# Moving VectorE's read of a finished projection chunk ahead of the recurrence's piece of the same step

## The chip, the cores and the metric

The kernel runs on one core of one Trainium2 chip. The metric is the device time of one execution in microseconds, the median of several runs.

## The reference

One inference step of a hybrid decoder layer, for a prompt of 1024 tokens and eight sample tokens, all in 32-bit floating point. One normalised input is projected into many features; they feed three branches whose outputs are merged, projected and followed by a feed-forward network.

```python
lru_x, lru_gate, q, cmp_kv, sel_kv, win_kv, ngate, mq, merge = project(x, p)
o_lru, conv_new, h_new = lru_branch(lru_x, lru_gate, ...)   # convolution, gates, scan over time
...
o_nsa = lax.map(block, jnp.arange(T // Q_BLOCK, dtype=jnp.int32))   # attention, 3 key sets
o_mem = mem_attend(mq, mkv)
y = merge_ffn(x, o_lru, o_nsa, o_mem, merge, p)
```

The recurrence is `h[t] = a[t] * h[t-1] + b[t]` for 1024 channels, where `a` and `b` come from two sigmoid gates of a four-tap convolution of `lru_x`; its output is multiplied by the GELU of `lru_gate`.

## The kernel before

The function `attention_and_recurrence` is the joined stage. It does three things at once, and every engine has its own instruction queue, written out in order for it.

- **Attention.** 192 steps, `J` = 0 to 191. A step is one head, one block of 128 queries and one of three key sets (`sel`, `win`, `cmp`). TensorE makes the scores of step J+1 (`scores`, tile `att_S`), later the transposes of the probabilities (`transposes`, `att_tp<-att_pr`) and the products with the values of the step before (`values`, `att_O`). VectorE adds the bias and takes the row maximum (`maxima`, `att_nmx`), gathers the output (`accumulate`) and makes the row's factor (`coefficient`). ScalarE makes the exponential (`probs`, `att_pr`), and behind it copies the transposed probabilities out of PSUM (`copies`, `att_ptr`).
- **Filler.** The projection's last 40 units of 128 features are worked off in between: each unit is three chunks, each chunk 24 matmuls into one PSUM bank (`facc`), cut into four ticks of six. `TICKS` says how many ticks a step holds: four (a whole chunk) in steps 0 to 71, one or two from 72 to 172. There is one bank, so the first matmul of a chunk waits until VectorE has read the chunk before it (`evict(g)`, line 1294, `att_zf<-att_facc`, which multiplies by the row's scale). `chunk_at[g]` is the step in which chunk g is finished.
- **Recurrence.** Four blocks of 256 channels. Each is cut into pieces, one a step at most, with steps between that have none: eight of the convolution (`convolve`, `att_xc`), then by number m: 1 and 2 gate times input, 3 and 4 the factor under the root, 6 and 7, 8 and 9 the scans (line 1382), 11 and 12 the output. ScalarE makes the sigmoids, exponentials, roots and GELU that pieces 1, 3, 6 and 11 wait for. The block's gate products on TensorE (`gate_products`, line 1064) wait for the whole convolution.

TensorE's order in step J is: `scores(J+1)`, gate products if any, the filler of step J, `values(J-1)`, `transposes(J)`. ScalarE's is: `probs(J+1)`, `copies(J)`, then weights, gates and its own piece of the recurrence. VectorE's, before, is: `evict` of the chunk that step J-1 finished, `maxima(J)`, `accumulate(J-2)`, `coefficient(J-1)`, the recurrence's piece of step J. In `cmp` steps of the first query block (2, 5, 8, 11, 14, 17, 20 and 23) the masked probabilities are made in `coefficient(J)`, in VectorE's step J+1, and `transposes(J)` waits for them. Steps 1 and 4 hold small instructions on the decay rates (lines 1270 to 1287) where a piece would stand. In steps 12, 41 and 70 the last piece of a block's convolution runs, and in the step behind each of these TensorE has that block's first gate products.

Of the kernel before, what the change touches and what calls it, by code (L numbers as in the profile page):

```python
# [742 lines left out]
def attention_and_recurrence(nc, d, per, h_hi, h_lo):  # L743
# [10 lines left out]
    NU = len(UNITS)  # L754
# [3 lines left out]
    def at(J):  # L758
        b, j = J // NJ, J % NJ
        return b, b // 2, j // NH, HALF[j % NH]  # L760

    def tiles(J):
        _, qt, _, (_, br) = at(J)
        return {"sel": (0, qt + 1), "win": (max(0, qt - 4), min(qt + 1, 5)), "cmp": (0, 1)}[br]
# [29 lines left out]
    chunk_at = {t // 4: J for J in ticks for t in ticks[J] if t % 4 == 3}  # L794
# [3 lines left out]
    for n in range(NBLK):  # L798
        W.append(max(unit_at[4 * n + 1] + 4, free))
        e, J = 0, W[n] + 11  # L800
# [11 lines left out]
    LAST = max(NST + 2, END)  # L812

    with ExitStack() as ctx:
# [439 lines left out]
        def _(dve):  # L1254
            chains, lams = [0], [0]

            def chain(ins):
                chains[0] += 1
                ins.then_inc(s_ch, 1)
                dve.wait_ge(s_ch, chains[0])  # L1260
# [6 lines left out]
            def decay_begin():  # L1267
                L = par[:, :, L_LAM]
                dve.wait_ge(par_in, 32)
                lam_chain(dve.tensor_scalar(lam[:, 0], L, -1.0, None, ALU.mult))  # L1270
                lam_chain(dve.tensor_tensor(lam[:, 1], L, lam[:, 0], ALU.max))
                dve.tensor_scalar(lam[:, 2], lam[:, 0], 0.0, None, ALU.max).then_inc(lam_done, 1)

            def decay_rates():
                dve.wait_ge(lam_ex, 1)
                lam_chain(dve.tensor_scalar(lam[:, 4], lam[:, 3], 2.0, None, ALU.add))
                lam_chain(dve.reciprocal(lam[:, 4], lam[:, 4]))
                lam_chain(dve.tensor_tensor(lam[:, 4], lam[:, 3], lam[:, 4], ALU.mult))
                lam_chain(dve.tensor_tensor(lam[:, 5], lam[:, 4], lam[:, 4], ALU.mult))
                lam_chain(dve.memset(lam[:, 6], 1.0 / 19))  # L1280
                for x in range(17, 0, -2):
                    lam_chain(dve.tensor_tensor(lam[:, 6], lam[:, 6], lam[:, 5], ALU.mult))
                    lam_chain(dve.tensor_scalar(lam[:, 6], lam[:, 6], 1.0 / x, None, ALU.add))
                lam_chain(dve.tensor_tensor(lam[:, 6], lam[:, 6], lam[:, 4], ALU.mult))
                lam_chain(dve.scalar_tensor_tensor(lam[:, 6], lam[:, 6], 2.0, lam[:, 2], ALU.mult, ALU.add))
                lam_chain(dve.tensor_scalar(lam[:, 6], lam[:, 6], -8.0, None, ALU.mult))
                dve.tensor_scalar(lam[:, 7], lam[:, 6], -1.0, None, ALU.mult).then_inc(lam_done, 1)

            def evict(g):
                u, c = g // 3, g % 3  # L1290
                if g >= 4:
                    dve.wait_ge(f_out[g % 4], 16 * (g // 4))
                dve.wait_ge(f_mm, g + 1)
                dve.tensor_tensor(zf[:, g % 4], facc[:, 0:CW], per["rstd"][:, c * CW:(c + 1) * CW],  # L1294
                                  ALU.mult).then_inc(f_ev, 1)

            def maxima(J):
                b, qt, s, (g, br) = at(J)
                x, n, rr = S[J % 2], width(J), 2 * (b % 2) + s
                if J % NH == 0:  # L1300
                    gt = per["gate"][:, qt, :].rearrange("p (g r c) -> p g r c", g=G, r=R)
                    chain(dve.tensor_copy(gsl[:, s], gt[:, :, rr, :]))
                dve.wait_ge(s_mm, J + 1)
                if br == "cmp":
                    c0 = 56 - 8 * qt
                    f = max(0, 40 - c0)
                    chain(dve.tensor_tensor(x[:, f:n], x[:, f:n], cstrip[:, g, rr, c0 + f - 40:c0 + n - 40], ALU.add))
                else:
                    m = min(n, 2 * P)
                    chain(dve.tensor_tensor(x[:, n - m:n], x[:, n - m:n], near[:, g, rr, 2 * P - m:], ALU.add))  # L1310
                    if br == "win" and qt >= 4:
                        chain(dve.tensor_tensor(x[:, 0:P], x[:, 0:P], wmask[:], ALU.add))
                dve.tensor_reduce(nmx[:, J % 2:J % 2 + 1], x[:, 0:n], AX, ALU.max, negate=True).then_inc(s_max, 1)  # L1313

            def coefficient(J):
                _, qt, s, (g, br) = at(J)
                bi = ("cmp", "sel", "win").index(br)
                v = rs[:, J % 2:J % 2 + 1]
                dve.wait_ge(s_exp, J + 1)
                if br == "cmp" and qt == 0:  # L1320
                    pm = pr[:, J % 2, 0:NCMP]
                    dve.tensor_tensor(pm, pm, cmask[:], ALU.mult).then_inc(s_pm, 1)  # L1322
                    dve.wait_ge(s_pm, J // 3 + 1)
                    chain(dve.tensor_reduce(v, pm, AX, ALU.add))
                    chain(dve.tensor_scalar(v, v, 1e-30, None, ALU.max))
                chain(dve.reciprocal(cf[:, J % 2, 0:1], v))
                chain(dve.tensor_tensor(cf[:, J % 2, 1:2], cf[:, J % 2, 0:1], gsl[:, s, g, bi:bi + 1], ALU.mult))

            def accumulate(J):
                _, _, s, (g, br) = at(J)  # L1330
                dve.wait_ge(s_pvg, vgroup(J + 1, 0))
                o = oacc[:, s, g * HD:(g + 1) * HD]
                c = cf[:, J % 2, 1:2]
                if br == "sel":
                    dve.tensor_scalar(o, O[:, 0:HD], c, None, ALU.mult).then_inc(s_acc, 1)
                else:
                    dve.wait_ge(s_acc, J)
                    dve.scalar_tensor_tensor(o, O[:, 0:HD], c, o, ALU.mult, ALU.add).then_inc(s_acc, 1)
# [20 lines left out]
            def recurrence(n, k, m):  # L1359

                if 2 <= k <= 9:
                    convolve(n, k - 2)
                if m in (1, 2):
                    t = m - 1
                    dve.wait_ge(sg_done, n + 1)
                    dve.tensor_tensor(ig[:, t], ig[:, t], xc[:, t], ALU.mult).then_inc(u_done, 1)
                if m in (3, 4):
                    t = m - 3
                    dve.wait_ge(a2_done, 2 * n + t + 1)
                    dve.scalar_tensor_tensor(e_[:, t], r[:, t], 1.0, e_[:, t], ALU.add, ALU.mult).then_inc(th_done, 1)  # L1370
                if m in (6, 7):
                    t = m - 6
                    dve.wait_ge(rt_done, n + 1)
                    dve.wait_ge(u_done, 2 * n + t + 1)
                    dve.tensor_tensor(ig[:, t], ig[:, t], e_[:, t], ALU.mult).then_inc(b_done, 1)
                if m in (8, 9):
                    t = m - 8
                    dve.wait_ge(b_done, 2 * n + t + 1)
                    dve.tensor_tensor(r[:, t, NP_:T], a[:, t, NP_:T], st[:, 2 * n + t, 3 * NS:], ALU.mult).then_inc(hs_done, 1)
                    dve.wait_ge(hs_done, 2 * n + t + 1)  # L1380
                    dve.tensor_tensor(r[:, t, NP_:T], r[:, t, NP_:T], ig[:, t, NP_:T], ALU.add)
                    dve.tensor_tensor_scan(r[:, t, 0:NP_], a[:, t, 0:NP_], ig[:, t, 0:NP_], 0.0, ALU.mult, ALU.add).then_inc(sc_done, 1)
                if m in (11, 12):
                    t = m - 11
                    dve.wait_ge(gl_done, n + 1)
                    dve.wait_ge(sc_done, 2 * n + t + 1)
                    dve.tensor_tensor(ig[:, t], r[:, t], e_[:, t], ALU.mult).then_inc(y_done, 1)
# [10 lines left out]
            chain(dve.tensor_copy(cstrip[:].rearrange("p g r n -> p (g r) n")[:, :, 0:24],  # L1398
                                  strip.rearrange("p h (n x) -> p h n x", x=16)[:, :, :, 0]))
            for J in range(LAST):  # L1400
                for g in range(3 * NU):
                    if chunk_at[g] + 1 == J and J:
                        evict(g)
                if J < NST:
                    maxima(J)
                if 2 <= J < NST + 2:
                    accumulate(J - 2)
                if 1 <= J <= NST:
                    coefficient(J - 1)
                if J == 1:  # L1410
                    decay_begin()
                if J == 4:
                    decay_rates()
                for n in range(NBLK):
                    recurrence(n, J - W[n], J - SIG[n])
            for g in range(3 * NU):
                if chunk_at[g] + 1 >= LAST:
                    evict(g)


# [1150 lines left out]
```

## Time and profile before

| | us |
|---|---|
| median of 3 runs | 2594.26 (2590.0 to 2599.5) |
| profiled execution | 2596.29 |
| its span, first to last instruction | 2594.6 |
| mean granted TensorE clock | 0.951 |
| TensorE busy | 2391.7 |
| VectorE busy | 1098.1 |
| ScalarE busy | 719.1 |

The profiled execution is one execution, 2.0 us above the median. Its span is what the views show; 1.7 us lie around it. Engines run side by side, so the busy times do not add up. The joined stage's steps 0 to 138 lie from 427.9 to about 1132 us of the span; the last recurrence piece is in step 137.

### The profile page before, as it was taken

What the parts mean: (1) busy time and instruction counts of PE and PEld (TensorE: products, weight loads), DVE (VectorE), ACT (ScalarE), POOL (GpSimd) and SP (SyncE); (2) the same over time, 40 slices, a digit from 0 to 9 for tenths busy, and PEclk for the clock granted to TensorE, in tenths of its full rate; (3) what the DMA queues carried; (4) which work ended last, traced back from release to release, by engine and by line L of the source; (5) the groups of instructions that cost most, each with busy time, mean ns of one, the idle gap of its engine ahead of it and who ended that gap; (6) DMA issues with size and microseconds to landing.
All of it is one profiled execution on the core that took longest, in us unless ns stands there. A gap on an engine that the chain in (4) does not pass through costs nothing. (4 is left out here: it accounts for less than half of the span.)

```text
span 2594.6 us, 37768 instructions
## 1 busy us (share of the span) xinstructions
PE 2391.7 (92%) x14375; PEld 2186.5 (84%) x14375; DVE 1098.1 (42%) x1981; ACT 719.1 (28%) x1319; POOL 648.9 (25%) x388
## 2 busy tenths in 40 slices
PE   7997777889989989989967899799999999999999
PEld 7996547878889778889856576799999999999999
DVE  5465013525336374465436221663333333333333
ACT  5222012133243544544334100432211111111111
POOL 2112102112211011111004120135443434434343
PEclk9998699999989999999868999899999999999999
DMA  5223506225534131120035332642111111111112
GB/s 178 88 80 133 177 29 191 63 70 177 135 84 116 39 100 40 42 88 29 20 110 132 122 114 90 220 147 98 42 49 42 49 40 49 43 46 49 40 49 81
DMA packets 135963, 226.31 MB, mean 87 GB/s; under 512 B 30842, under 2 KB 93946, under 8 KB 135228
## 3 DMA queue, kind: packets, MB, share of 16 engines
q1 hardware_dynamic: 118172, 191.50, 24.2%
q0 software_dynamic: 5376, 21.00, 2.4%
q10 hardware_dynamic: 12288, 12.06, 1.6%
q8 instruction: 85, 1.39, 0.2%
q14 instruction: 42, 0.34, 0.0%
HBM read 176.80 MB, written 55.08 MB: 89 GB/s over the span
## 5 line engine op out<-in xcount | busy, mean ns | idle before, releaser
L1114 PE MATMUL att_facc<-h_hi,att_w_hi 128*128 128x344 f32 x960 | 338.3, 352 | 57.3 <-DVE att_zf L1294 44.2
L1114 PE MATMUL att_facc<-h_hi,att_w_lo 128*128 128x344 f32 x960 | 315.1, 328 | 0.0
L1114 PE MATMUL att_facc<-h_lo,att_w_hi 128*128 128x344 f32 x960 | 315.0, 328 | 0.0
L2275 PE MATMUL tl_acc<-tl_x_hi,up_w_hi 128*128 128x344 f32 x1248 | 266.1, 322 | 16.1 <-DVE tl_x_lo L2338 13.6
L2275 PE MATMUL tl_acc<-tl_x_lo,up_w_hi 128*128 128x344 f32 x1248 | 265.7, 321 | 0.0
L2275 PE MATMUL tl_acc<-tl_x_hi,up_w_lo 128*128 128x344 f32 x1248 | 264.0, 320 | 0.0
L2240 POOL TENSOR_TENSOR up_w_lo<-up_raw,up_w_hi 128x1024 fp32r<-128x1024 f32 x64 | 154.0, 2407 | 424.9 <-ACT up_w_hi L2180 424.9
L1114 PEld LDWEIGHTS att_facc<-h_hi,att_w_hi 128*128 128x128 f32 x960 | 188.3, 196 | 71.8 <-DVE att_zf L1294 41.9
L1152 ACT ACTIVATE att_pr<-att_S,att_nmx 128x63 f32<-128x63 f32 (+8 forms) x192 | 110.0, 573 | 474.1 <-DVE att_nmx L1313 473.8
L1009 POOL TENSOR_TENSOR att_w_lo<-att_raw,att_w_hi 128x1024 fp32r<-128x1024 f32 x40 | 98.0, 2450 | 558.9 <-ACT att_w_hi L1147 558.9
L2392 DVE TENSOR_TENSOR up_z<-tl_acc,up_z 128x1032 f32<-128x1032 f32 x176 | 217.0, 1233 | 47.8 <-PE tl_acc L2325 46.8
L2180 ACT ACTIVATE up_w_hi<-up_raw 128x1024 fp32r<-128x1024 f32 x64 | 68.0, 1062 | 597.4 <-PE tl_acc L2275 390.6
L2275 PEld LDWEIGHTS tl_acc<-tl_x_hi,up_w_hi 128*128 128x128 f32 x1248 | 210.1, 188 | 17.3 <-issue 16.9
L2275 PEld LDWEIGHTS tl_acc<-tl_x_lo,up_w_hi 128*128 128x128 f32 x1248 | 212.0, 190 | 0.0
L2275 PEld LDWEIGHTS tl_acc<-tl_x_hi,up_w_lo 128*128 128x128 f32 x1248 | 208.5, 188 | 0.0
L1114 PEld LDWEIGHTS att_facc<-h_lo,att_w_hi 128*128 128x128 f32 x960 | 188.7, 197 | 8.1 <-issue 7.7
L1114 PEld LDWEIGHTS att_facc<-h_hi,att_w_lo 128*128 128x128 f32 x960 | 187.8, 196 | 0.0
L1294 DVE TENSOR_TENSOR att_zf<-att_facc,h_rstd 128x344 f32<-128x344 f32 x120 | 61.8, 515 | 293.9 <-PE att_facc L1114 293.5
L1077 PE MATMUL att_tp<-per_ident,att_pr 128*128 128x128 f32 x592 | 108.1, 297 | 15.8 <-DVE att_pr L1322 15.8
L2325 PE MATMUL tl_acc<-up_x_hi,up_w_hi 128*128 128x344 f32 x528 | 121.4, 338 | 0.0
L2388 DVE TENSOR_TENSOR tl_tmp<-tl_acc,tl_tmp 128x1032 f32<-128x1032 f32 x22 | 27.1, 1233 | 220.9 <-PE tl_acc L2275 214.7
L1164 ACT ACTIVATE att_ptr<-att_tp 63x128 f32<-63x128 f32 (+4 forms) x256 | 98.5, 410 | 67.7 <-PE att_tp L1077 67.1
(375 smaller groups left out, 4494.0 us busy)
## 6 DMA issues: line engine op xcount, KB each, us to landing
up_raw<-in_w_ff SPq DMA_DIRECT2D x66, 512.0 KB, 3.6
z<-att_zf SPq DMA_DIRECT2D x120, 172.0 KB, 4.1
att_raw<-in_w_in SPq DMA_DIRECT2D x40, 512.0 KB, 4.2
tl_tmp<-z SPq DMA_DIRECT2D x24, 516.0 KB, 6.0
fr_raw<-in_w_in SPq DMA_DIRECT2D x14, 512.0 KB, 4.8
zn<-fr_x SPq DMA_DIRECT2D x10, 516.0 KB, 2.9
fr_x<-in_xT SPq DMA_DIRECT2D x8, 644.0 KB, 10.4
up_raw<-in_w_up ACTq DMA_DIRECT2D x10, 512.0 KB, 3.7
```

Of the source, the lines that this page charges most:

```text
L1009: pool.tensor_tensor(w_lo[:, u % 2], raw[:, u % 2], w_hi[:, u % 2].bitcast(F32), ALU.subtract).then_inc(f_lo, 1)
L1077: mm = pe.transpose(tp[tg % 2][:, (t % 4) * P:(t % 4 + 1) * P], pr[:, J % 2, t * P:(t + 1) * P], per["ident"][:])
L1114: mm = pe.matmul(facc[:, 0:CW], w[:, u % 2, k, :], h[:, k, c * CW:(c + 1) * CW], start=(x == 0), stop=(x == 23))
L1152: act.activation(pr[:, J % 2, 0:n], S[J % 2][:, 0:n], ACT.Exp, bias=nmx[:, J % 2:J % 2 + 1], accum_out=rs[:, J % 2:J % 2 + 1]).then_inc(s_ ...
L1164: act.activation(ptr[0:w, vg % 4, 0:m], tp[tg % 2][0:w, 0:m], ACT.Copy).then_inc(s_te, 1)
L1294: dve.tensor_tensor(zf[:, g % 4], facc[:, 0:CW], per["rstd"][:, c * CW:(c + 1) * CW], ALU.mult).then_inc(f_ev, 1)
L2180: act.activation(w_hi[:, u % 2], raw[:, u % 2], ACT.Copy).then_inc(whi_done, 1)
L2240: pool.tensor_tensor(w_lo[:, u % 2], raw[:, u % 2], w_hi[:, u % 2].bitcast(F32), ALU.subtract).then_inc(wlo_done, 1)
L2275: mm = pe.matmul(a[:, c, 0:CW], wt[:, s, k, :], x[:, x0, c * CW:(c + 1) * CW], start=first and n == 0, stop=last and n == 2)
L2325: mm = pe.matmul(acc[m % 2][:, c, 0:CW], wt[:, j, m, :], x[:, j, c * CW:(c + 1) * CW], start=(n == 0), stop=(n == 2))
L2388: dve.tensor_tensor(gj, acc[1][:, :, 0:CW], gj, ALU.mult).then_inc(ev_done, 1)
L2392: dve.tensor_tensor(chunks(h[:, m]), acc[m % 2][:, :, 0:CW], chunks(h[:, m]), ALU.add).then_inc(ev_done, 1)
```

## The change

VectorE's read of a chunk moves from the beginning of step J+1 to step J itself, between `coefficient(J-1)` and the recurrence's piece (or the decay instructions). Since nothing else stands between the end of step J and the beginning of step J+1, only the piece is passed.

```diff
             for J in range(LAST):
-                for g in range(3 * NU):
-                    if chunk_at[g] + 1 == J and J:
-                        evict(g)
                 if J < NST:
                     maxima(J)
                 if 2 <= J < NST + 2:
                     accumulate(J - 2)
                 if 1 <= J <= NST:
                     coefficient(J - 1)
+                for g in range(3 * NU):
+                    if chunk_at[g] == J:
+                        evict(g)
                 if J == 1:
                     decay_begin()
                 if J == 4:
                     decay_rates()
                 for n in range(NBLK):
                     recurrence(n, J - W[n], J - SIG[n])
             for g in range(3 * NU):
-                if chunk_at[g] + 1 >= LAST:
+                if chunk_at[g] >= LAST:
                     evict(g)
```

Of the 114 chunks that are finished in steps 0 to 172, 57 end in a step with a piece or decay instructions, and for these the order changes; for the other 57 it is what it was. The other engines' queues do not change.

VectorE's queue around step 8, a `cmp` step of the first query block with a piece of the convolution (lines 1356 and 1357); `att_pr` in line 1322 are the masked probabilities of step 8. Before:

```order
L1327 TENSOR_TENSOR att_cf<-att_cf,att_gsl 128x1
L1356 SCALAR_TENSOR_TENSOR att_xc<-att_xp,att_par,att_xc 128x1024
L1357 SCALAR_TENSOR_TENSOR att_xc<-att_xp,att_par,att_xc 128x8
L1294 TENSOR_TENSOR att_zf<-att_facc,h_rstd 128x344
L1310 TENSOR_TENSOR att_S<-att_S,att_near 128x128
L1313 TENSOR_REDUCE att_nmx<-att_S 128x1
L1338 SCALAR_TENSOR_TENSOR att_oacc<-att_O,att_cf,att_oacc 128x64
L1322 TENSOR_TENSOR att_pr<-att_pr,att_cmask 128x63
```

The same place now:

```order
L1327 TENSOR_TENSOR att_cf<-att_cf,att_gsl 128x1
L1294 TENSOR_TENSOR att_zf<-att_facc,h_rstd 128x344
L1356 SCALAR_TENSOR_TENSOR att_xc<-att_xp,att_par,att_xc 128x1024
L1357 SCALAR_TENSOR_TENSOR att_xc<-att_xp,att_par,att_xc 128x8
L1310 TENSOR_TENSOR att_S<-att_S,att_near 128x128
L1313 TENSOR_REDUCE att_nmx<-att_S 128x1
L1338 SCALAR_TENSOR_TENSOR att_oacc<-att_O,att_cf,att_oacc 128x64
L1322 TENSOR_TENSOR att_pr<-att_pr,att_cmask 128x63
```

The chunk's read (line 1294) has passed the convolution's two instructions; these now stand between it and the next step's maxima and mask.

VectorE's queue around step 57, which holds piece 6 of block 1 (line 1375, behind ScalarE's square root). Before:

```order
L1327 TENSOR_TENSOR att_cf<-att_cf,att_gsl 128x1
L1375 TENSOR_TENSOR att_ri<-att_ri,att_e 128x1032
L1294 TENSOR_TENSOR att_zf<-att_facc,h_rstd 128x344
L1310 TENSOR_TENSOR att_S<-att_S,att_near 128x256
L1313 TENSOR_REDUCE att_nmx<-att_S 128x1
```

Now:

```order
L1327 TENSOR_TENSOR att_cf<-att_cf,att_gsl 128x1
L1294 TENSOR_TENSOR att_zf<-att_facc,h_rstd 128x344
L1375 TENSOR_TENSOR att_ri<-att_ri,att_e 128x1032
L1310 TENSOR_TENSOR att_S<-att_S,att_near 128x256
L1313 TENSOR_REDUCE att_nmx<-att_S 128x1
```

Here the read no longer stands behind an instruction that waits for ScalarE, and the maxima of step 58 still do.

## Rows read from the trace of the kernel before

**Rows 1.** The page: busy time, share of the span, instructions, of TensorE.

```profile
PE 2391.7 (92%) x14375; PEld 2186.5 (84%) x14375; DVE 1098.1 (42%) x1981; ACT 719.1 (28%) x1319; POOL 648.9 (25%) x388
```

**Rows 2.** TensorE's waits (total us, times, longest) in 427.9:560, 560:847.6, 847.6:1139 in turn.

```profile
PE att_tp L1077 <- DVE att_pr L1322: 10.3, 7, 1.6
...
PE att_facc L1114 <- DVE att_zf L1294: 13.6, 7, 4.0
...
PE att_facc L1114 <- DVE att_zf L1294: 19.1, 7, 5.7
...
PE att_O L1096 <- ACT att_ptr L1164: 6.3, 9, 1.2
```

**Rows 3.** Busy time by stretch, instructions, granted clock, DMA share, GB/s.

```profile
core 0: us, PE busy (x) PEld busy (x) DVE busy (x) ACT busy (x) POOL busy (x), PEclk, DMA share, GB/s
...
560.00:847.60 287.60, 268.48 (x1658) 252.22 (x1658) 136.14 (x377) 108.15 (x229) 58.26 (x48) 0.96 0.44 122
...
847.60:1139.00 291.40, 265.75 (x1700) 238.08 (x1699) 163.23 (x441) 149.39 (x323) 33.02 (x21) 0.96 0.21 64
```

**Rows 4.** Timeline, step 57: start, us, engine, line, operation [idle before].

```profile
766.22 0.32 PE L1114 MATMUL att_facc<-h_hi,att_w_lo 128*128 128x344 f32 x1
...
768.78 1.23 DVE L1375 TENSOR_TENSOR att_ri<-att_ri,att_e 128x1032 f32<-128x1032 f32 x1 [5.15 <-ACT att_e L1207]
...
770.49 0.66 PE L1114 MATMUL att_facc<-h_hi,att_w_hi 128*128 128x344 f32 x1 [2.96 <-DVE att_zf L1294]
...
771.97 0.48 ACT L1164 ACTIVATE att_ptr<-att_tp 128x384 f32<-128x384 f32 x1
...
776.88 0.55 PE L1096 MATMUL att_O<-att_v_sel,att_ptr 128*128 128x64 f32 x4
```

**Rows 5.** Timeline after steps 33 and 52: ScalarE's copy, TensorE's value products.

```profile
630.17 0.37 ACT L1164 ACTIVATE att_ptr<-att_tp 128x256 f32<-128x256 f32 x1
...
634.34 0.55 PE L1096 MATMUL att_O<-att_v_sel,att_ptr 128*128 128x64 f32 x4
...
741.40 0.48 ACT L1164 ACTIVATE att_ptr<-att_tp 128x384 f32<-128x384 f32 x1
...
746.67 0.55 PE L1096 MATMUL att_O<-att_v_win,att_ptr 128*128 128x64 f32 x4
```

**Rows 6.** Timeline after step 81, where the next filler is two ticks long.

```profile
896.92 0.65 PE L1114 MATMUL att_facc<-h_hi,att_w_hi 128*128 128x344 f32 x1 [5.65 <-DVE att_zf L1294]
...
898.64 0.59 ACT L1164 ACTIVATE att_ptr<-att_tp 128x512 f32<-128x512 f32 x1
...
900.53 0.73 PE L1096 MATMUL att_O<-att_v_sel,att_ptr 128*128 128x64 f32 x3
```

**Rows 7.** Timeline of step 8: convolution, chunk read, masked probabilities, transpose.

```profile
472.86 1.28 DVE L1356 SCALAR_TENSOR_TENSOR att_xc<-att_xp,att_par,att_xc 128x1024 f32<-128x1024 f32 x1
...
474.06 0.22 DVE L1357 SCALAR_TENSOR_TENSOR att_xc<-att_xp,att_par,att_xc 128x8 f32<-128x8 f32 x1
...
476.17 0.52 DVE L1294 TENSOR_TENSOR att_zf<-att_facc,h_rstd 128x344 f32<-128x344 f32 x1 [1.88 <-PE att_facc L1114]
...
477.59 0.33 PE L1077 MATMUL att_tp<-per_ident,att_pr 128*128 128x128 f32 x1 [1.37 <-DVE att_pr L1322]
```

**Rows 8.** Timeline of step 13: the recurrence's first gate products.

```profile
498.11 0.68 PE L1064 MATMUL att_S<-att_xc,att_wa 128*128 128x512 f32 x1
```

**Rows 9.** VectorE by line, 427.9:1139: busy us, mean ns of one, idle before.

```profile
L1382 DVE TENSOR_TENSOR_SCAN att_ri<-att_xp,att_ri 128x1024 f32<-128x1024 f32 x8 | 18.3, 2284 | 0.0
```

**Rows 10.** Timeline after step 134, a scan step: copy and value products.

```profile
1119.25 0.26 ACT L1164 ACTIVATE att_ptr<-att_tp 63x128 f32<-63x128 f32 x1
...
1119.65 0.40 PE L1096 MATMUL att_O<-att_v_cmp,att_ptr 63*128 63x64 f32 x2 [0.42 <-ACT att_ptr L1164]
```

**Rows 11.** Two fillers, 24 matmuls each: after waits of 2.48 and 1.57 us.

```profile
455.00:460.40 5.40, 5.40 (x24) 5.40 (x25) 1.74 (x7) 0.58 (x3) 0.00 (x0) 0.68 0.17 38
...
493.50:497.40 3.90, 3.90 (x27) 3.73 (x25) 3.79 (x5) 1.22 (x2) 2.49 (x1) 1.00 0.00 0
```

## The prediction

> **What bounds the kernel now.** I began with the page: TensorE is busy for 92% of the span [rows 1], so a change on VectorE can give or take only what TensorE waits. The change touches steps 1 to 136, and I asked next for TensorE's waits in three stretches of these (steps 0 to 21, 22 to 71, 72 to 138). The reader sees three kinds [rows 2]. TensorE waits for the read of the last chunk (13.6 and 19.1 us in the second and third stretch): that is what the change can remove. In the first it waits for masked probabilities (10.3 us, the `cmp` steps). And in the third it waits for ScalarE's copies (6.3 us), the other end of the chain maxima, exponential, copy. The granted clock in the last two stretches is 0.96 [rows 3], so low-clock time is small but there. Then I read the timeline at single steps, since each moved read has its own answer: what stood behind it, and which wait ends last afterwards.
>
> **What the change removes.** It adds no instruction; what counts is what the read no longer waits for, and what now waits for the read.
>
> Step 57 is the clear case. The filler's last matmul starts at 766.22, but VectorE stands until 768.78 before a piece that waits for ScalarE's root (5.15 us idle); the read comes behind it, and TensorE starts the next filler at 770.49 after 2.96 us [rows 4]. Afterwards the read comes at about 766.7, and TensorE goes on at 770.49 - 2.96 = 767.5. A filler of four ticks takes 3.9 us at full clock [rows 11], so it ends at 771.4. Then the value products need ScalarE's copy, behind the exponential and the maxima, and these are still behind the piece. They come only 0.42 us earlier, since the read (0.52 us, the next instruction 0.43 behind it) is no longer ahead of them: the copy ended at 771.97 + 0.48 = 772.45 and will end at 772.0. The products start at 772.05 instead of 776.88 [rows 4]: **4.8 us**, of which 2.5 are not the wait itself but the filler at half clock behind it.
>
> The same with steps 33 and 52: copies end at 630.54 and 741.88, less 0.42; the products started at 634.34 and 746.67 [rows 5]. That is 4.2 and 5.2 us. The other waits of this stretch are 13.6 less the three long ones (2.98, 3.96, 2.96), so 3.7 us; the four-tick filler covers the chain behind them, and I take them whole. Step 23, where the transposes wait anyway, gives the 0.4 of the read. Second stretch: **18.1 us given back**.
>
> In the third stretch a filler is one or two ticks, so it hides much less of the same chain. At step 81 the wait is 5.65 us, but the copy ended at 899.23 and the products started at 900.53 [rows 6]: 900.53 - 898.85 = 1.7 us is all that is won, and the rest becomes a wait for ScalarE. Read in the same way, the other five places with a long wait (steps 86, 91, 126, 131 and 136) give 1.6, 2.4, 0.5, 0.5 and 1.0. Third stretch: **7.7 us**, 0.4 of its 19.1.
>
> **What it adds.** The read waits for TensorE's filler of the same step, and the piece is behind it in VectorE's queue. Before, the piece ran in the time in which VectorE had nothing to do (idle 1.88 us before the read at step 8, with the piece done [rows 7]); that cover is gone. The piece now starts after the filler's end, and the maxima, the mask and the gate products wait for it. Four prices follow.
>
> (a) Steps 5, 8 and 11: the transposes wait for the mask made behind the piece. At step 8 TensorE waited 1.37 us, from the read at 476.17 to 477.59; the piece (474.06 + 0.22 - 472.86 = 1.42 us) comes in between [rows 7]. So 1.4 us each at 8 and 11, with waits of 2.8 and 3.0 us. After a wait of 2.48 us the filler ran at a mean clock of 0.68 for 5.4 us (partly at 1.2 instead of 2.4 GHz), and after one of 1.57 us at 1.00 [rows 11]: (1 - 0.68) x 5.4 = 1.7 us lost. Waits of 2.8 to 3.0 us are on the far side, so I add 1.7 us to each: 6.2 us. At steps 4 and 5 the decay instructions (28 small ones in step 4, some 5 us) move behind the read: the filler starts 2.5 us sooner and then waits as much behind them, at both places without work, for 1.5 us more of low clock. Sum 7.7 us.
>
> (b) Steps 12, 41 and 70: gate products in the next step wait for the convolution. The first starts at 498.11 [rows 8]; the filler of step 12 ends at 497.5, then read and piece take 0.5 + 1.4 us, so 499.5. 1.4, 1.4 and, with longer transposes ahead, 0.8: 3.6 us.
>
> (c) The scans, 2.28 us and with their small instructions 2.6 [rows 9]. In four-tick steps the copy ended 2.0 to 2.3 us before the value products began, so 0.3 to 0.6 is left over, at steps 30, 59 and 60: 1.3 us. Other pieces (1.2 to 1.5 us) fit under the filler in these steps, about thirty times, at no cost. If that cover were 1 us shorter, each would cost up to 0.5 us.
>
> (d) In the third stretch pieces fit less well. At step 134 the copy ended at 1119.51 and the products began at 1119.65 [rows 10]; the scan ran while the filler did and now starts behind it, 1.6 us later. That is 1.4 us. Steps 83, 88, 93, 95 and 129, read alike, give 0.8, 1.0, 1.3, 0.85 and 0.25. Sum 5.6 us.
>
> The Trainium skill ("TensorE: Matmul & The Clock Gate", "Architectural detail: the array is 16× 32×32, not 1× 128×128", on queue depths) says that VectorE and ScalarE are strict first-in, first-out, while TensorE may at most pull weight loads ahead. That speaks against this change: by this rule a read that waits for TensorE also holds a piece whose inputs are ready. The trace agrees, with reads behind waiting pieces in every case above.
>
> **Sum.** First stretch: 7.7 + 1.4 = 9.1 us longer. Second: 18.1 - (1.4 + 0.8 + 1.3) = 14.6 shorter. Third: 7.7 - 5.6 = 2.1 shorter. In all 7.6 us shorter, against the profiled execution of 2596.29: 2588.7. That one is 2.0 us above the median, so on the median 2594.26 it is 2586.7; I say **2587**. What follows step 138 has its own order and moves along as it is.
>
> **The rivals.**
>
> *The clock doesn't fall in steps 8 and 11* and the small pieces cost nothing. For it: a low stretch is not certain, after 1.57 us there was none [rows 11]. Then 3.4 of (a), 1.5 of steps 4 and 5 and some 3 us of (d) are not lost: 15 to 16 us shorter, 2579. Chance 0.17.
>
> *The wait only moves.* TensorE stands as long for ScalarE's copies as it did for the read. For it: this is what step 81 shows, and 70% of the third stretch. Against it: steps 33, 52 and 57, where a filler of 3.9 us lies between. It would need the long fillers to gain only their waits (9.9 instead of 14.2) and 3 us more of (d): within 1 us of no change, 2594. Chance 0.20.
>
> *Slower: pieces without cover.* The one mechanism is (c) with a cover that is too short: VectorE's queue after a filler's end is read 0.5, piece 1.5, maxima 0.5 to 1.1, then exponential and copy, and the next read is due one filler later. If these about thirty-five steps lose 0.5 us each, it is 17 us against the 7.6: 2604. It decides from 0.2 us a step. Against it: the copies are 2.0 us or more ahead there, and the piece takes 1.5. Chance 0.11.
>
> *The change does nothing* cannot be: 57 reads change place.
>
> **How the numbers follow.** The forecast has 0.52, with a range of its own from 2581 to 2592 (the clock at steps 5, 8 and 11 both ways, the third stretch half as large or twice). A measurement of this kernel can tell about 0.3% from no change, that is 7.8 us: below 2586.5 is faster. That line runs through the middle of my forecast: 0.26 of it is faster, 0.26 the same. With the first rival faster is 0.43; with the second, and none from the third, same is 0.46; slower is 0.11. The range for 8 in 10 takes in the first rival and the second whole and leaves the third out: 2577 to 2599.
>
> **What the profile after would show.** If right: TensorE's waits for the chunk's read in the second stretch fall from 13.6 to under 2 us; in the third from 19.1 to under 4, while the waits for ScalarE's copies rise from 6.3 to some 17. Waits for the masked probabilities in the first stretch rise from 10.3 to 13 or more, with two or three waits near 3 us and low clock behind them. From step 0 to step 22 it takes 9 us longer, from there to step 72 15 us less, and from there to step 138 2 us less. If the low clock is missing there, the first rival holds. If the second stretch gives less than 10 us, the step that failed is the cover of ScalarE's chain by the long filler. The prediction is wrong above all if ScalarE's own pieces, which I moved along with the rest, come to stand between exponential and copy.

## The result, and the profile after

| | before | after |
|---|---|---|
| median of 20 runs each, on one chip | 2594.89 (2590.0 to 2602.92) | **2603.74** (2593.98 to 2611.09) |
| ratio | | **1.0032** (95%: 1.0022 to 1.0042) |
| profiled execution; its span | 2596.29; 2594.6 | 2599.66; 2598.0 |

The change makes the kernel 8.9 us slower; the forecast was 7.6 us faster. The profiled execution of after lies 4.1 us below the median of its kernel, that of before 1.4 us above its own. So the two profiles differ by only 3.4 us, and a reading of the whole spans would hide most of the loss.

The page's line of busy times, beside [rows 1]:

```profile
PE 2386.9 (92%) x14375; PEld 2179.8 (84%) x14375; DVE 1101.6 (42%) x1981; ACT 718.1 (28%) x1319; POOL 651.9 (25%) x388
```

TensorE is busy for 4.8 us less than before, and the span is 3.4 us longer: it waits more. Where, is told by the windows, cut at the first filler matmul of steps 0, 22, 72 and 138 (width; busy us by engine; granted clock; DMA share and GB/s):

```profile
core 0: us, PE busy (x) PEld busy (x) DVE busy (x) ACT busy (x) POOL busy (x), PEclk, DMA share, GB/s
429.21:567.34 138.13, 119.69 (x688) 107.88 (x688) 49.80 (x201) 27.94 (x90) 21.85 (x12) 0.96 0.27 77
567.34:849.73 282.39, 265.27 (x1660) 247.08 (x1659) 144.73 (x377) 108.31 (x229) 60.55 (x48) 0.99 0.44 126
849.73:1140.03 290.30, 263.37 (x1649) 236.59 (x1648) 157.83 (x427) 145.40 (x313) 31.07 (x21) 0.94 0.19 58
```

The same steps took 132.05, 287.63 and 283.37 us before. The last column of the next table is half of the time in which the clock records stand at 0.5 (1.2 instead of 2.4 GHz), that is what the low clock costs at most.

| steps | before | after | difference | forecast | low clock, before and after |
|---|---|---|---|---|---|
| 0 to 21 | 132.05 | 138.13 | +6.1 | +9.1 | 3.4, 5.1 |
| 22 to 71 | 287.63 | 282.39 | -5.2 | -14.6 | 11.9, 3.4 |
| 72 to 137 | 283.37 | 290.30 | +6.9 | -2.1 | 11.9, 17.1 |
| sum | 703.05 | 710.82 | +7.8 | -7.6 | |

The rest of the 3.4 us lies where the order is that of before: the start lies 1.2 us later, and steps 174 to 190 took 57.54 us instead of 63.41, at a granted clock of 0.79 instead of 0.66.

Each of these lengths is from one profile. How far they scatter is told by the profiles of the experiments below, where several kernels have one VectorE order in a stretch. The first took 130.5 to 132.1 us in eight with the order of before, and 137.7 to 138.1 in after, e2, e5 and e7, which move the reads that the forecast prices there. The third took 281.1 to 287.0 us in seven with the order of before (low clock 11.9 to 17.1 us), and 289.5 to 290.4 in three with that of after. So the third stretch is longer for sure, but by how much is uncertain by some 3 us.

TensorE's waits in the same three stretches, in turn (total us, times, longest), beside [rows 2]:

```profile
PE att_tp L1077 <- DVE att_pr L1322: 13.3, 7, 2.9
...
PE att_O L1096 <- ACT att_ptr L1164: 10.5, 11, 2.0
...
PE att_facc L1114 <- DVE att_zf L1294: 0.2, 1, 0.2
...
PE att_O L1096 <- ACT att_ptr L1164: 26.7, 14, 5.6
```

The waits for the chunk's read are gone, 13.6 and 19.1 us before and 0.2 and none now. In their place TensorE waits for ScalarE's copies: 10.5 us in the second stretch, where there was no such wait before, and 26.7 in the third.

Step 57, timeline, beside [rows 4] (start, us, engine, line, operation, idle before):

```profile
768.77 0.40 PE L1114 MATMUL att_facc<-h_hi,att_w_hi 128*128 128x344 f32 x1
...
770.13 1.23 DVE L1375 TENSOR_TENSOR att_ri<-att_ri,att_e 128x1032 f32<-128x1032 f32 x1 [1.53 <-ACT att_e L1207]
...
772.91 0.48 ACT L1164 ACTIVATE att_ptr<-att_tp 128x384 f32<-128x384 f32 x1
...
773.53 0.63 PE L1096 MATMUL att_O<-att_v_sel,att_ptr 128*128 128x64 f32 x4 [0.75 <-ACT att_ptr L1164]
```

This went as forecast. The next filler starts at 768.77 without a wait, and the value products start 0.14 us behind the copy's end (773.39). From the filler's start of step 57 to these products it took 14.26 us before and 9.50 now: 4.8 us. Steps 33 and 52 [rows 5], measured alike, give 4.1 and 5.1.

Step 8, beside [rows 7]:

```profile
479.21 0.52 DVE L1294 TENSOR_TENSOR att_zf<-att_facc,h_rstd 128x344 f32<-128x344 f32 x1 [2.04 <-PE att_facc L1114]
...
479.65 1.28 DVE L1356 SCALAR_TENSOR_TENSOR att_xc<-att_xp,att_par,att_xc 128x1024 f32<-128x1024 f32 x1
...
481.70 0.21 DVE L1322 TENSOR_TENSOR att_pr<-att_pr,att_cmask 128x63 f32<-128x63 f32 x1
...
481.98 0.48 PE L1077 MATMUL att_tp<-per_ident,att_pr 128*128 128x128 f32 x1 [2.73 <-DVE att_pr L1322]
```

The convolution runs between the read and the mask, and the wait for the mask is 2.73 us instead of 1.37.

### The profile page after: what moved, and what is told of

The parts are those of the page before. It is cut to its first block and busy times, and to the rows that moved or that the text cites. A ratio compares the mean times of both kernels' runs of the same rounds, so it can differ in the third digit from the quotient of the medians.

```text
span 2598.0 us, 37726 instructions
## 1 busy us (share of the span) xinstructions
PE 2386.9 (92%) x14375; PEld 2179.8 (84%) x14375; DVE 1101.6 (42%) x1981; ACT 718.1 (28%) x1319; POOL 651.9 (25%) x388
## 5 line engine op out<-in xcount | busy, mean ns | idle before, releaser
L1114 PEld LDWEIGHTS att_facc<-h_hi,att_w_hi 128*128 128x128 f32 x960 | 186.9, 195 | 35.1 <-POOL att_w_lo L1009 13.6
L1077 PE MATMUL att_tp<-per_ident,att_pr 128*128 128x128 f32 x592 | 107.5, 295 | 18.3 <-DVE att_pr L1322 18.3
```

What stands on the lines that cost most here:

```text
L1077: mm = pe.transpose(tp[tg % 2][:, (t % 4) * P:(t % 4 + 1) * P], pr[:, J % 2, t * P:(t + 1) * P], per["ident"][:])
L1114: mm = pe.matmul(facc[:, 0:CW], w[:, u % 2, k, :], h[:, k, c * CW:(c + 1) * CW], start=(x == 0), stop=(x == 23))
```

## Experiments

Each kernel ran beside the kernel before on the same chip; the ratio has its 95% interval. A step in `early` is one in which the read goes ahead of the piece; in all others the order is that of before:

```diff
                 for g in range(3 * NU):
-                    if chunk_at[g] + 1 == J and J:
+                    if chunk_at[g] + 1 == J and J and J - 1 not in early:
                         evict(g)
...
                     coefficient(J - 1)
+                for g in range(3 * NU):
+                    if chunk_at[g] == J and J in early:
+                        evict(g)
```

The expectations name two theories of the loss. The collision theory: a moved piece meets GpSimd's subtraction and is stretched by it. The cover theory: the chain of piece, maxima, exponential and copy is too long for the filler, with or without GpSimd.

### The change in two halves

```diff
+            early = {SIG[n] + m for n in range(NBLK) for m in (1, 6, 11)}
```

These are the twelve steps whose piece waits for ScalarE (`e1_scalar_pieces`).

> The read goes ahead of the piece only in the 12 steps whose piece waits for ScalarE (m = 1, 6 and 11 of each block); everywhere else it is as before. Both theories say that the gains of the changed kernel are made here and its losses elsewhere: 17 to 19 us less from step 22 to step 72, up to 8 us less behind it, so 15 to 25 us less than before in all. If instead the gains were taken back by waits for ScalarE that follow later, it would be within 5 us of before.

Measured: 2574.84 us against 2593.58, ratio 0.993 (0.9917 to 0.9943), 18.7 us faster. The second stretch took 273.46 us, 14.2 less than before, where the gains of the forecast come to 18.1. Of the missing 3.9, 3.3 lie behind steps 34 and 63, which hold two pieces ahead of the read in this kernel: against after, it starts the next filler 1.2 and 2.1 us later there. The third took 281.63, only 1.7 less, where the forecast had 7.7. TensorE's waits in the third stretch of this kernel:

```profile
PE att_O L1096 <- ACT att_ptr L1164: 21.1, 12, 5.6
PE att_facc L1114 <- DVE att_zf L1294: 0.6, 1, 0.6
```

The 19.1 us for the read have become waits for ScalarE's copies.

```diff
+            early = set(range(LAST)) - {SIG[n] + m for n in range(NBLK) for m in (1, 6, 11)}
```

The complement (`e2_other_pieces`).

> The complement: the read goes ahead in the other 45 steps alone. Collision theory and cover theory both expect a slower kernel, by what the changed kernel lost and e1 won together: 9 + 20 = 25 to 30 us more than before. If it is less than 12 us more, losses and gains do not add up and something else is at work.

Measured: 2609.19 us against 2593.58, ratio 1.0064 (1.0051 to 1.0078), 15.6 us slower, where both theories had 25 to 30: the halves, -18.7 and +15.6, come to -3.1 in sum, and the whole change is +8.9. By stretches it lost 5.8, 9.1 and 5.8 us against before. The first and the third are near what (a), (b) and (d) say. In the second the forecast has 3.5 us for steps 41, 70 and the scans, and everything else there at no cost.

### What makes the pieces longer

In the profile of after, step 36's convolution shows it (GpSimd is POOL):

```profile
646.48 2.38 POOL L1009 TENSOR_TENSOR att_w_lo<-att_raw,att_w_hi 128x1024 fp32r<-128x1024 f32 x1 [11.70 <-ACT att_w_hi L1147]
...
646.64 0.52 DVE L1294 TENSOR_TENSOR att_zf<-att_facc,h_rstd 128x344 f32<-128x344 f32 x1 [1.50 <-PE att_facc L1114]
...
647.07 2.87 DVE L1356 SCALAR_TENSOR_TENSOR att_xc<-att_xp,att_par,att_xc 128x1024 f32<-128x1024 f32 x1
...
649.86 0.21 DVE L1357 SCALAR_TENSOR_TENSOR att_xc<-att_st,att_par,att_xc 128x8 f32<-128x8 f32 x1
...
650.45 0.42 DVE L1313 TENSOR_REDUCE att_nmx<-att_S 128x1 f32<-128x256 f32 x1
...
651.37 0.37 ACT L1164 ACTIVATE att_ptr<-att_tp 128x256 f32<-128x256 f32 x1
...
651.89 0.63 PE L1096 MATMUL att_O<-att_v_sel,att_ptr 128*128 128x64 f32 x4 [0.63 <-ACT att_ptr L1164]
```

GpSimd starts its subtraction on the filler's weights (line 1009) at 646.48. VectorE's read beside it keeps its 0.52 us, but the convolution takes 2.87 us instead of 1.28 and ends at 649.94, 1.09 us behind GpSimd's end. Maxima, exponential and copy come that much later, and TensorE waits 0.63 us. The same place before:

```profile
641.34 1.28 DVE L1356 SCALAR_TENSOR_TENSOR att_xc<-att_xp,att_par,att_xc 128x1024 f32<-128x1024 f32 x1
...
642.65 2.38 POOL L1009 TENSOR_TENSOR att_w_lo<-att_raw,att_w_hi 128x1024 fp32r<-128x1024 f32 x1 [14.49 <-ACT att_w_hi L1147]
...
644.12 0.52 DVE L1294 TENSOR_TENSOR att_zf<-att_facc,h_rstd 128x344 f32<-128x344 f32 x1 [1.35 <-PE att_facc L1114]
...
644.55 0.42 DVE L1310 TENSOR_TENSOR att_S<-att_S,att_near 128x256 f32<-128x256 f32 x1
```

There the convolution was through when GpSimd began, VectorE then waited for the filler, and what ran beside GpSimd was the read and the bias, both from PSUM, at their usual length. VectorE's lines in after show the sum (busy us, mean ns of one, idle before):

```profile
L1356 DVE SCALAR_TENSOR_TENSOR att_xc<-att_xp,att_par,att_xc 128x1024 f32<-128x1024 f32 x24 | 37.2, 1552 | 0.1
...
L1382 DVE TENSOR_TENSOR_SCAN att_ri<-att_xp,att_ri 128x1024 f32<-128x1024 f32 x8 | 18.3, 2284 | 0.0
...
L1370 DVE SCALAR_TENSOR_TENSOR att_e<-att_ri,att_e 128x1032 f32<-128x1032 f32 x8 | 11.4, 1422 | 0.1
...
L1387 DVE TENSOR_TENSOR att_ri<-att_ri,att_e 128x1032 f32<-128x1032 f32 x8 | 11.3, 1417 | 3.0 <-ACT att_e L1210 2.9
```

The means before were 1285, 2284 [rows 9], 1234 and 1232 ns. The Trainium skill ("SBUF — State Buffer", "Who interferes with whom") states that a VectorE instruction with two SBUF inputs contends with a GpSimd instruction that reads SBUF, and that whichever starts first blocks the other wholly, while one with at most one SBUF input does not contend outside the 2-port modes. The trace agrees: the convolution has two inputs in SBUF and is held for all of GpSimd's instruction; the read has one, the other being in PSUM. The other way round is in the trace too. Here a scan, also with two inputs in SBUF, started 0.45 us ahead of the subtraction:

```profile
784.55 2.28 DVE L1382 TENSOR_TENSOR_SCAN att_ri<-att_xp,att_ri 128x1024 f32<-128x1024 f32 x1
...
785.00 4.03 POOL L1009 TENSOR_TENSOR att_w_lo<-att_raw,att_w_hi 128x1024 fp32r<-128x1024 f32 x1 [15.28 <-ACT att_w_hi L1147]
```

The scan kept its 2.28 us, and GpSimd's subtraction took 4.03 us instead of 2.38. The scans' mean did not move.

Two kernels were to move GpSimd's subtraction off the pieces, one on after and one on before:

```diff
                     if unit_at[u - 2] == J:
+                        if J < 6 * NJ:
+                            pool.wait_ge(s_max, J + 3)
                         w_low(u)
```

> The changed kernel, with GpSimd's subtraction of each unit's weights held back in steps 0 to 71 until the row maxima of step J+2 are done, so that it does not run beside a moved piece. Collision theory: VectorE's long pieces are no longer stretched (none over 1.5 us between steps 22 and 72), and that stretch is 8 to 12 us shorter than in the changed kernel, so 8 to 12 us less in all. Cover theory (the chain piece, maxima, exponential, copy is too long for the filler with or without GpSimd): within 3 us of the changed kernel.

> The same delay of GpSimd's subtraction in the kernel before, as a control. Both theories: within 4 us of before, since there the pieces run ahead of the subtraction. If it is as much faster as e3, the delay helps for another reason.

Measured: 2601.85, ratio 1.0039 (1.0025 to 1.0053), and 2608.97, ratio 1.0058 (1.0045 to 1.0071), both against 2593.58. The second stretch of the first took 282.74 us, no less than after's 282.39. The control, which should have stayed within 4 us of before, lost 15.4. The delayed subtraction had found another victim: the small product of the coefficient (line 1327 in before), which has two SBUF inputs too, took 2.2 instead of 0.16 us 23 times in each of these two kernels. So here too the length goes by what lies beside GpSimd, but nothing can be read from the pair about the change.

So the subtraction itself was made small, in after and in before. From unit 2 on it covers 8 elements a partition instead of 1024, so the low part of the filler's weights is left out:

```diff
-                pool.tensor_tensor(w_lo[:, u % 2], raw[:, u % 2], w_hi[:, u % 2].bitcast(F32), ALU.subtract).then_inc(f_lo, 1)
+                k, m = (KT, P) if u < 2 else (1, 8)
+                pool.tensor_tensor(w_lo[:, u % 2, 0:k, 0:m], raw[:, u % 2, 0:k, 0:m],
+                                   w_hi[:, u % 2, 0:k, 0:m].bitcast(F32), ALU.subtract).then_inc(f_lo, 1)
```

> The changed kernel with GpSimd's subtraction cut to 8 columns from the third unit on; it leaves out the low part of these weights, so TensorE works on old values in the same matmuls. Collision theory: no long piece of VectorE is stretched from step 22 to 72, and this stretch takes 270 to 274 us instead of 282.4. Cover theory: 279 us or more, since ScalarE's chain is as long as it was.

> The same cut in the kernel before. Both theories: step 22 to step 72 within 4 us of the 287.6 of before, since there GpSimd runs mostly beside reads of PSUM. So with e5 the change should win 5 us or more as a whole by the collision theory (forecast of the prediction: 7.6), and lose as it did by the cover theory.

Measured: 2590.56, ratio 0.9984 (0.9972 to 0.9997), and 2583.2, ratio 0.9951 (0.9939 to 0.9963), both against 2593.82. Second and third stretch of the first of them, by windows:

```profile
567.39:840.43 273.04, 262.93 (x1659) 245.52 (x1659) 132.10 (x377) 108.03 (x229) 22.94 (x48) 0.99 0.43 128
840.43:1130.85 290.42, 263.67 (x1649) 236.64 (x1648) 150.69 (x424) 144.96 (x312) 11.45 (x21) 0.94 0.19 58
```

Its convolution and its pieces of lines 1370 and 1387 (two lines lower here), and its waits for the copies in the second stretch:

```profile
L1358 DVE SCALAR_TENSOR_TENSOR att_xc<-att_xp,att_par,att_xc 128x1024 f32<-128x1024 f32 x24 | 31.4, 1307 | 0.1
...
L1389 DVE TENSOR_TENSOR att_ri<-att_ri,att_e 128x1032 f32<-128x1032 f32 x8 | 10.0, 1249 | 4.4 <-ACT att_e L1212 4.3
...
L1372 DVE SCALAR_TENSOR_TENSOR att_e<-att_ri,att_e 128x1032 f32<-128x1032 f32 x8 | 9.8, 1226 | 0.1
```

```profile
PE att_O L1098 <- ACT att_ptr L1166: 2.9, 6, 1.0
```

The second stretch takes 273.04 us instead of after's 282.39, the means are back at 1307, 1249 and 1226 ns, and the waits for the copies fall from 10.5 to 2.9 us. In before the same edit gives 285.75 instead of 287.63. So with the small subtraction the change gives 12.7 us in this stretch (forecast 14.6), with the real one 5.2: **7.5 us** is what the interference takes. In the third stretch it explains nothing: 290.42 in this kernel against 290.30 in after. And it does not decide the sign: with the small subtraction on both sides the change still costs 2590.56 - 2583.2 = 7.4 us, 1.5 less than the 8.9 with the real one. The collision theory had the change win 5 us or more as a whole; so it was right for the second stretch and wrong for the whole kernel.

### The terms one at a time

```diff
+            early = {4, 5, 8, 11, 12, 41, 70}
...
+            early = {SIG[n] + m for n in range(2) for m in (1, 6, 11)}
```

The first line is that of e7, the second that of e8.

> The read goes ahead only in steps 4, 5, 8, 11, 12, 41 and 70: the mask and gate prices alone, (a) and (b) of the prediction, 11.3 us together. Both theories: 8 to 13 us slower than before, 6 to 9 of it ahead of step 22. If the low clock behind the two waits near 3 us is only chance, 4 to 8.

> e1 without its six steps behind step 72: the read goes ahead in steps 23, 28, 33, 52, 57 and 62 alone. Both theories: 14 to 18 us faster than before. With e1's 18.7 us the difference shows what the six late steps are worth: 2 to 5 us if most of the wait turns into a wait for ScalarE there, as forecast for step 81; 8 or more if the whole wait were won.

Measured, against 2593.82: 2604.09, ratio 1.0034 (1.0021 to 1.0046), 10.3 us slower; and 2579.59, ratio 0.994 (0.9927 to 0.9952), 14.2 us faster. By the medians the price of the seven steps is about right (11.3 forecast). By stretches e7 is 5.6, 4.7 and 2.6 us longer than before, where the forecast has 9.1, 2.2 and none; the 2.6 lie where its order is that of before. The six waiting pieces of blocks 0 and 1 carry three quarters of what all twelve give; the six in the third stretch are worth 18.7 - 14.2 = 4.5 us by the medians, and 1.7 to 1.9 by the profiles' windows (281.63 against 283.37 and 283.50).

```diff
+            early = {J for J in range(72, LAST)} - {SIG[n] + m for n in range(NBLK) for m in (1, 6, 11)}
...
+            early = ({J for J in range(22, 72)} - {SIG[n] + m for n in range(NBLK) for m in (1, 6, 11)}) - {41, 70}
```

The first line is that of e9, the second that of e10. A third kernel, `e11_second_other_small`, is e10 with the small subtraction, and leaves out the same part of the weights as above.

> The read goes ahead only behind step 72 and only where the piece does not wait for ScalarE (steps 83, 88, 93, 95, 97, 129 and 134; price (d) of the prediction, 5.6 us). Theory that only the pieces' own time is uncovered: 4 to 7 us slower than before. Theory that TensorE's new waits of 1.75 to 2 us bring low clock as well, four spells of 1.7 us: 8 to 13 us slower, with 3 us or more of additional low-clock loss between step 72 and 138.

> The read goes ahead only from step 23 to 69 where the piece does not wait for ScalarE, without 41; the prediction gave these 1.3 us. Collision theory: 8 to 12 us slower than before, all of it between steps 22 and 72. If the pieces fit under the filler as predicted: within 3 us of before.

> e10 with GpSimd's subtraction cut to 8 columns as in e6, its control at 2583.2 us; it leaves out the low part of these weights. Collision theory: within 3 us of e6. Cover theory: as much slower than e6 as e10 is slower than before.

Measured, against 2595.32: e9 2591.46, ratio 0.9986 (0.9977 to 0.9995); e10 2600.49, ratio 1.0019 (1.0003 to 1.0035); e11 2589.94, ratio 0.9973 (0.9964 to 0.9982). e10 is 5.2 us slower by the medians, less than the 8 to 12 expected. But its second stretch took 297.68 us, 10.1 more than before, from steps that the forecast prices at 1.3 us together. TensorE's waits in it:

```profile
PE att_facc L1114 <- DVE att_zf L1294: 12.4, 6, 4.0
PE att_O L1096 <- ACT att_ptr L1164: 7.6, 8, 1.6
```

The waits for the read stay, since the waiting pieces are where they were, and 7.6 us of waits for the copies are added. With the small subtraction the same order takes 286.90 us against 285.75 (e6), 1.1 us more. This is the plainest evidence: the pieces do fit under the filler, as long as GpSimd is not beside them. As a whole e11 is 6.7 us slower than e6, though (1.5 of it in the runs of before on its chip), which its moved steps don't account for: 3.8 us of it lie in the third stretch of the two profiles, where both have the order of before.

In e9 the third stretch and steps 174 to 190 read:

```profile
850.01:1139.37 289.36, 259.86 (x1650) 232.81 (x1648) 156.63 (x426) 145.53 (x313) 31.05 (x21) 0.96 0.19 58
1277.64:1333.18 55.54, 45.70 (x284) 41.92 (x285) 26.11 (x86) 23.92 (x65) 1.46 (x2) 0.83 0.03 7
```

The third stretch is 6.0 us longer than before, as term (d) has it (5.6), without more low clock (11.9 us in both). The second of its two theories had four more spells of low clock there, and none came. And yet the kernel as a whole is 3.9 us faster by the medians. Steps 174 to 190, whose order is the same in all these kernels, took 55.54 us here and 63.41 in before, at a granted clock of 0.83 instead of 0.66. Whether a change in the stretch ahead brings this about, or it is chance, one profile each can't tell.

### A better version

The piece that waits for ScalarE can be moved and the read left where it is: VectorE's pieces m = 1, 6 and 11 are done one step later, together with 2, 7 and 12.

```diff
-                if m in (6, 7):
-                    t = m - 6
+                if m == 7:
                     dve.wait_ge(rt_done, n + 1)
-                    dve.wait_ge(u_done, 2 * n + t + 1)
-                    dve.tensor_tensor(ig[:, t], ig[:, t], e_[:, t], ALU.mult).then_inc(b_done, 1)
+                    dve.wait_ge(u_done, 2 * n + 2)
+                    for t in range(2):
+                        dve.tensor_tensor(ig[:, t], ig[:, t], e_[:, t], ALU.mult).then_inc(b_done, 1)
```

and pieces 1 and 2, and 11 and 12, likewise.

> The kernel before, with its order of the read, but the pieces m = 1, 6 and 11 of each block run one step later, together with m = 2, 7 and 12. VectorE then has no reason to stand before ScalarE's result with a chunk's read and the next row maxima behind it. If the cause of TensorE's long waits is this queueing alone, both the read and the maxima are on time: faster than e1 by another 4 to 12 us, 2562 to 2571 us. If ScalarE itself, busy with its own piece, is what TensorE waits for, it is within 4 us of e1 (2575).

Measured: **2563.43** against 2593.54, ratio 0.9887 (0.9868 to 0.9906), 30 us faster than before and 11.4 faster than e1. Windows of the three stretches:

```profile
432.26:562.82 130.56, 116.69 (x687) 105.28 (x688) 55.00 (x201) 27.90 (x90) 22.30 (x12) 0.99 0.29 84
562.82:829.90 267.08, 261.68 (x1659) 245.87 (x1659) 136.51 (x377) 107.66 (x229) 59.09 (x48) 0.99 0.46 131
829.90:1104.17 274.27, 257.27 (x1650) 230.25 (x1648) 158.74 (x426) 145.11 (x313) 31.08 (x21) 0.96 0.20 61
```

Its waits in the second and the third:

```profile
PE att_facc L1114 <- DVE att_zf L1294: 2.9, 3, 2.4
...
PE att_O L1096 <- ACT att_ptr L1164: 0.6, 1, 0.6
...
PE att_O L1096 <- ACT att_ptr L1164: 16.2, 13, 4.6
```

Some wait for the read is left, 2.9 us, but in the third stretch the waits for the copies are 16.2 us instead of e1's 21.1: the maxima no longer stand behind a waiting piece either.

## Why the prediction was wrong

Between the first filler of step 0 and that of step 138 the forecast had 7.6 us less, and the profiles have 7.8 more. The first stretch came out 3.0 us better than forecast, the second 9.4 worse and the third 9.0 worse.

**Right: what the read waited for, and the gains at it.** Steps 33, 52 and 57 gave 4.1, 5.1 and 4.8 us (forecast 4.2, 5.2 and 4.8), and TensorE's waits for the read fell as told. Adding up each filler start of the second stretch that came sooner against before gives 18.7 us (forecast 18.1, though its own terms, 4.8, 4.2, 5.2, 3.7 and 0.4, add up to 18.3); those that came later, 13.5 (forecast 3.5).

**Right in mechanism, somewhat dear: (a) and (b).** The longest waits for the mask are 2.9 and 2.73 us, and the 2.2 us that the filler starts sooner behind step 4 came back as a wait of 2.4 us. Low clock followed at steps 5 and 8, with spells of 6.8 and 3.4 us. Steps 4 and 5 together cost 1.7 us (forecast 1.5), step 8 2.9 (3.1), step 11 1.4 (3.1, no low clock), the gate products behind step 12 1.5 (1.4): 7.5 us instead of 9.1. That the stretch as a whole is only 6.1 us longer has another reason: before has a low-clock spell at 554.2, behind the wait for the mask of step 20, worth 1.5 us, which after, e2, e5 and e7 don't have. Seven of the eight profiles with the order of before in these steps have it, so it seems to go with that order; why, is open.

What did not hold is the premise, "Waits of 2.8 to 3.0 us are on the far side". The wait of 2.93 us at step 11 had no low clock behind it, in after and in e2, e5 and e7 alike. And [rows 11]'s own case, a wait of 2.46 to 2.49 us ahead of step 5's filler in eight kernels, had low clock behind it in before, e6 and e8 and none in e1, e9, e10, e11 and e12. The forecast priced low clock at steps 8 and 11 as certain, and it came at 8 alone.

**The step that failed: (c), "Other pieces (1.2 to 1.5 us) fit under the filler in these steps, about thirty times, at no cost".** I looked at how long the pieces take and how long the filler covers them, and didn't ask what runs beside the pieces at their new place. Before, VectorE did them while it would else have been idle, and met GpSimd's subtraction mostly with instructions that read PSUM. Now they begin 0.43 us behind the read, and some meet it. A few of them pay, as the filler starts of after and e5 show, set side by side: after is later by 1.5 us at the start of step 32's filler, 0.9 at 38, 0.9 at 41, 0.8 at 56, 2.8 and 0.5 at 65 and 66, 1.3 at 68 and 0.8 at 71. That is 9.5 us (7.5 net of what the small subtraction gives before), for the most part from pieces two steps ahead of each (at 65 up to 1.7 of the 2.8 us is a low-clock spell behind the longer wait, at 806.2): the value products that wait for the copy stand between. The cause is shown by e5 and e6, and by e10 and e11, in which 10.1 us become 1.1. The forecast's own guard named this outcome, "If the second stretch gives less than 10 us, the step that failed is the cover of ScalarE's chain by the long filler". The cover fell short because the piece was longer, and not because the filler was shorter.

**Mis-sized: the third stretch, -2.1 us forecast, +6.9 measured.** Term (d) was right within the scatter: 5.6 forecast, 6.0 in e9. The gain of 7.7 us was not: e1 shows 1.7, and the medians of e1 and e8 4.5. Step 81 in after, beside [rows 6]:

```profile
898.65 0.59 ACT L1164 ACTIVATE att_ptr<-att_tp 128x512 f32<-128x512 f32 x1
...
899.38 1.94 PE L1096 MATMUL att_O<-att_v_sel,att_ptr 128*128 128x64 f32 x8 [5.64 <-ACT att_ptr L1164]
...
902.82 0.49 PE L1114 MATMUL att_facc<-h_hi,att_w_hi 128*128 128x344 f32 x1
...
903.11 0.49 PE L1114 MATMUL att_facc<-h_lo,att_w_hi 128*128 128x344 f32 x1
```

The products start 1.6 us sooner after the filler of step 81 than before, as forecast (1.7); the same in e1. But before, the low clock behind the wait fell on the filler of step 82, and that of step 83 had full clock again, 2.04 us for its 12 matmuls. Now TensorE does filler 82 first, then waits 5.64 us, and the low clock falls on the products and on filler 83: its matmuls start 0.29 us apart instead of 0.16. In e1 filler 83 takes 3.63 us, and at the start of filler 84 nothing of the 1.7 us is left; the kernel is 0.8 us behind there. Step 126 went the same way: 1.1 us won, 2.0 lost within two steps. I had counted only up to the value products, and carried no cost for the clock behind a wait that stays. Low clock in the third stretch is 11.9 us before, 13.7 in e1 and 17.1 in after; of the 6.9 us that this stretch took longer, up to 5.2 are low clock. That share is weak evidence, since e4 has 17.1 with the order of before there. What makes after's 17.1 out of e1's 13.7 and e9's 11.9 stays open: the additions of e9 alone cost 6.0 us, on top of e1 8.7.

**The rivals.** *The wait only moves* is what the third stretch did, and more than that; the 70% that the prediction gives for the stretch is step 81's share, by its own sum it is 60%. *Pieces without cover* gives 2604, within 0.3 us of the result, but that is chance: it had 0.5 us at thirty-five steps, and the runs show 0.5 to 2.8 us at eight, no cover missing elsewhere (e11), and the rest of the loss in the third stretch. *The clock doesn't fall* holds at step 11 alone. The check that I set, that ScalarE's copies would take up the waits from 6.3 to some 17, went to 26.7.

**What does not add up.** In the stretches where they moved reads, e1, e7, e9 and e10 together give +5.6, +0.6 and +4.3 us against before, 10.5 in sum; the change gives +6.1, -5.2 and +6.9, 7.8 in sum. By medians it is worse: -18.7, +10.3, -3.9 and +5.2, in sum -7.1, against +8.9 measured, as the two halves gave -3.1. So each term's mechanism is read from its steps, and the sizes are good to a few microseconds only. The difference lies in part in steps 174 to 190, 55.5 to 64.5 us long in kernels with one order there.

## What to carry to other kernels

When an instruction is moved in a queue, look up what every other engine does at its new time, GpSimd above all: an instruction with both inputs in SBUF that is moved off idle time may wait for the rest of a GpSimd instruction that began before it. Follow a gain past the wait that it removes to the end of the next two steps, since low clock that followed the wait before can follow the one that takes its place. And if one instruction in a queue waits long, move that one and leave those that don't: the twelve waiting pieces one step later gave 30 us, where the read ahead of every piece cost 9.

## What the runs showed of the hardware

- VectorE instructions as small as 128x1 and 128x8 are held too. In before, at the place below, one that usually takes 0.16 us takes 1.26 beside a subtraction of GpSimd from 921.73 to 924.10; a `TENSOR_SCALAR` of 128x8 with one SBUF tensor took 2.33 instead of 0.28 us beside another, at 801.95.

```profile
922.86 1.26 DVE L1327 TENSOR_TENSOR att_cf<-att_cf,att_gsl 128x1 f32<-128x1 f32 x1
```

- It goes both ways: in before, GpSimd's subtraction that started at 609.46 beside a scan running from 608.44 took 3.4 us instead of 2.38, and the scan its usual 2.28.
- The length of one wait of TensorE did not settle whether low clock followed. None followed a wait of 2.93 us until 500.55 in after, one of 1.94 until 788.86 in e1 and one of 1.76 until 602.02 in before; it did follow waits of 1.75 us until 935.73 and of 1.94 until 1129.10, both in after.
- Executions of kernels with the same order in steps 174 to 190 differ there by up to 9 us, with the granted clock of these steps between 0.63 (e10, 64.50 us) and 0.83 (e12, 55.50 us).
